# A three-product split of the first mixer's output projection on one Trainium2 core

## The reference, cut to what matters

```
def bidirectional(h, s_f0, s_b0):
    q, k, v, r, g_f, g_b = project(h)
    o_f, s_f = gla_chunk_scan(q, k, v, g_f, s_f0)
    o_b, s_b = gla_chunk_scan(flip_seq(q), flip_seq(k), flip_seq(v), flip_seq(g_b), s_b0)
    o = head_rms_norm(o_f + flip_seq(o_b), norm_g)
    return (o * jax.nn.silu(r)) @ w_out, s_f, s_b
...
lat = lat + (mod_l[:, 2] * rms_norm(y_lat, norm_g[i, 1])).astype(lat.dtype)
h = modulate(rms_norm(lat, norm_g[i, 2]), mod_l[:, 3], mod_l[:, 4])
lat = lat + (mod_l[:, 5] * rms_norm(swiglu(h, ffn_w_in[i], ffn_w_out[i]), norm_g[i, 3])).astype(lat.dtype)
```

## Time and profile before

| what | value |
|---|---|
| median of 3 runs | 1257.98 us (1257.1 to 1258.12) |
| the profiled execution's own time | 1255.89 us |
| its span, first to last instruction | 1253.6 us |
| mean granted TensorE clock | 0.989 of full speed |
| PE busy | 1190.9 us, 95% of the span |
| VectorE (DVE) busy | 730.1 us, 58% |
| ScalarE (ACT) busy | 538.2 us, 43% |
| GpSimd (POOL) busy | 38.7 us, 3% |
| HBM read | 207.86 MB, 167 GB/s over the span |

### The profile page before, as it was taken

How to read it: one execution, slowest core, us unless ns; L and a number is a source line. 1 busy time by engine, 2 the same in 40 slices (tenths; PEclk the granted TensorE clock), 3 DMA queues, 4 the chain that set the end, 5 groups by cost and what they waited for, 6 DMA issues and landing times.

```text
span 1253.6 us, 18595 instructions
## 1 busy us (share of the span) xinstructions
PE 1190.9 (95%) x7327; PEld 1009.3 (81%) x7327; DVE 730.1 (58%) x969; ACT 538.2 (43%) x715; POOL 38.7 (3%) x54
## 2 busy tenths in 40 slices
PE   3899998989999989999999999999999999999997
PEld 1477785479999978646899998999999985999996
DVE  1569335265555557664555456777777765654553
ACT  3762121253433453553343245555555544533442
POOL 2000010000000061000000000000000000000000
PEclk9998999999999989999999999999999999999999
DMA  9673470799655560425655543555555354746510
GB/s 319 235 275 107 167 268 7 246 244 281 199 156 150 184 172 5 184 85 197 208 198 176 200 110 107 146 152 151 151 147 134 76 200 160 256 154 206 179 65 34
DMA packets 201037, 209.70 MB, mean 167 GB/s; under 512 B 5803, under 2 KB 166838, under 8 KB 200790
## 3 DMA queue, kind: packets, MB, share of 16 engines
q1 hardware_dynamic: 197520, 201.61, 50.7%
q0 software_dynamic: 1648, 5.03, 1.6%
q10 hardware_dynamic: 1814, 2.30, 0.5%
HBM read 207.86 MB, written 2.01 MB: 167 GB/s over the span
## 4 chain that ended last, share of the span: by engine, by line
PE 87%; DVE 6%; DMA 3%; ACT 2%; issue 2%; DVEq 0%; SPq 0%; ACTq 0%
PE bank L1915 21%; PE bank L1916 20%; PE bank L1917 20%; PE bank L1713 3%; PE bank L1714 3%; PE bank L1715 3%; DMA weight_pool<-in_mod_w_dram 2%; PE bank L2129 2%; PE bank L1867 2%; PE bank L2270 2%; PE bank L2258 1%; PE bank L2248 1%; PE bank L1670 1%; DVE work L1435 1%; PE bank L2239 1%
## 5 line engine op out<-in xcount | busy, mean ns | idle before, releaser
L1915 PE MATMUL bank<-hT_high,mlp_up_high 128*128 128x256 f32 x512 | 145.2, 284 | 1.1 <-DVE hT_low L1337 1.1
L1917 PE MATMUL bank<-hT_high,mlp_up_low 128*128 128x256 f32 x512 | 144.9, 283 | 0.0
L1916 PE MATMUL bank<-hT_low,mlp_up_high 128*128 128x256 f32 x512 | 144.9, 283 | 0.0
L1915 PE MATMUL bank<-od_w_high,hT_high 128*128 128x384 f32 x384 | 132.7, 346 | 1.6 <-DVE hT_low L1337 1.4
L1917 PE MATMUL bank<-od_w_high,hT_low 128*128 128x384 f32 x384 | 128.7, 335 | 0.0
L1916 PE MATMUL bank<-od_w_low,hT_high 128*128 128x384 f32 x384 | 128.4, 334 | 0.0
L1041 DVE TENSOR_TENSOR mlp_down_low<-weight_pool,mlp_down_high 128x2048 fp32r<-128x2048 f32 x32 | 73.3, 2290 | 59.1 <-ACT mlp_down_high L620 59.1
L1915 PE MATMUL bank<-hT_high,ffn_up_high 128*128 128x256 f32 x352 | 99.8, 284 | 1.5 <-DVE hT_low L1041 1.5
L1915 PEld LDWEIGHTS bank<-hT_high,mlp_up_high 128*128 128x128 f32 x512 | 98.1, 192 | 2.9 <-issue 2.0
L1915 PE MATMUL bank<-mlp_down_high,hidden_high 128*128 128x512 f32 x256 | 99.9, 390 | 0.0
L1916 PE MATMUL bank<-mlp_down_low,hidden_high 128*128 128x512 f32 x256 | 99.9, 390 | 0.0
(11 more groups left out here) (311 smaller groups left out, 2589.7 us busy)
## 6 DMA issues: line engine op xcount, KB each, us to landing
weight_pool<-in_mlp_w_dram SPq DMA_DIRECT2D x64, 1024.0 KB, 7.5
weight_pool<-in_od_w_in_dram SPq DMA_DIRECT2D x72, 512.0 KB, 5.2
weight_pool<-in_mod_w_dram SPq DMA_DIRECT2D x22, 1024.0 KB, 9.8
weight_pool<-in_ffn_w_in_dram SPq DMA_DIRECT2D x44, 512.0 KB, 5.8
weight_pool<-in_gla_w_in_dram SPq DMA_DIRECT2D x12, 1024.0 KB, 6.5
weight_pool<-in_ffn_w_out_dram SPq DMA_DIRECT2D x22, 512.0 KB, 7.1
weight_pool<-in_gla_w_out_dram SPq DMA_DIRECT2D x2, 2048.0 KB, 15.4
weight_pool<-in_ev_w_in_dram SPq DMA_DIRECT2D x4, 1024.0 KB, 7.3
```

The lines of the kernel that those rows point to most:

```text
L1915: mm(out_, left[0], right[0], start=start, stop=False, **flag)
L1916: mm(out_, left[0], right[1], start=False, stop=False, **flag)
L1917: return mm(out_, left[1], right[0], start=False, stop=stop, **flag)
```

## The change

The output product takes the split form.

- **Activations.** `ogT` becomes `ogT2`, a high and a low half. ScalarE copies each of the banks 4 to 7 whole (512 columns) into the high half, VectorE subtracts for the low half.
- **Weights.** ScalarE makes the high halves of eight slices of 1024 columns: k 0 to 4 once the scores are done (`sT_ps` 4) and the weights have landed, k 5 to 7 after the last `state_updates` (`upd_ps` 8), since their place in `hT` holds `keT` until then. GpSimd makes the low halves of k 0 to 5, VectorE those of k 6 and 7. The low halves overwrite the raw weights.
- **Product.** 96 instructions with the same order of k and banks as before. PE waits for `ogT_lo`, `go_lo` and `go_lo_dve` in place of `ogT_act`, `ogT_dve` and the landings.
- **Places.** The two FFN weight sets change places (set 0 now at word 0), since the new halves lie in `work` at 8192 to 15360. So `ev_c` half 1 shares its place with the set of the last block, and is split after the last up product and no longer in the block before.

The diff, cut to its core, has in this order the places, GpSimd (ahead of `gate_rows(0)`), ScalarE (ahead of the squares, then the end of the FFN), VectorE (in place of `turn_evac`) and TensorE. Left out are the planner's entry that reserves words 16384 to 18431 of the pool for two high halves, VectorE's like edit at the end of the FFN, and `split_mm`, which only stands earlier in the code.

```
+        ogT2 = [view(over(f"mixed_{w}", "work", at, 2048), 0, KD, SEQ) for w, at in (("high", 8192), ("low", 12288))]
+        GO_HIGH = [("weight_pool", 16384), ("weight_pool", 17408), ("work", 10240), ("work", 11264), ("work", 14336), ("hT", 1024), ("hT", 2048), ("hT", 3072)]
+        goL = [over(f"gla_out{k}_low", "weight_pool", 8192 + D * k, D) for k in range(KD)]
...
-               for j, at in enumerate((10240, 0))]
+               for j, at in enumerate((0, 10240))]
...
+            for k in range(6):
+                g.wait_ge(s["go_hi"], k + 1)
+                e = L["go", k // 4]
+                g.tensor_tensor(goL[k][:, :], pool[:, e.at + D * (k % 4):e.at + D * (k % 4) + D], goH[k][:, :].bitcast(F32), ALU.subtract)\
+                 .then_inc(s["go_lo"], 1)
...
+            act.wait_ge(s["sT_ps"], 4)
+            for k in range(5):
+                gla_out_high(k)
+            act.wait_ge(s["upd_ps"], 8)
+            for k in range(5, KD):
+                gla_out_high(k)
...
-                if f >= FFC - 3 and f < FFC - 1:
-                    half = f - (FFC - 3)
+                if f == FFC - 3 or f == FFC - 1:
+                    half = (f - (FFC - 3)) // 2
                     if half:
-                        act.wait_ge(s["ff_ps"], FFC - 1)
+                        act.wait_ge(s["ff_ps"], FFC)
...
+            for k in (6, 7):
+                dve.wait_ge(s["go_hi"], k + 1)
+                e = L["go", 1]
+                low(goL[k][:, :], pool[:, e.at + D * (k - 4):e.at + D * (k - 4) + D], goH[k][:, :], "go_lo_dve")
+            for b in range(4):
+                dve.wait_ge(s["ogT_hi"], b + 1)
+                low(ogT2[1][:, 2 * b:2 * b + 2, :], bank[4 + b][:, :].rearrange("p (k t) -> p k t", k=2), ogT2[0][:, 2 * b:2 * b + 2, :], "ogT_lo")
...
-            out_product(0, [("go", 0), ("go", 1)], ogT)
+            for k in range(4):
+                pe.wait_ge(s["ogT_lo"], k // 2 + 1)
+                pe.wait_ge(s["go_lo"], k + 1)
+                for b in range(4):
+                    ins = out_part(k, b)
+            ins.then_inc(s["out_used"], 1)
+            pe.wait_ge(s["ogT_lo"], 4)
+            pe.wait_ge(s["go_lo"], 6)
+            pe.wait_ge(s["go_lo_dve"], 2)
+            for b in range(4):
+                for k in range(4, KD):
+                    ins = out_part(k, b)
+                if b == 1:
+                    ins.then_inc(s["y_half"], 1)
```

85 lines of the change are left out of this document (28 added, 57 removed).

## The result

The changed kernel takes 1249.10 us, median of 6 executions (1246.39 to 1251.43), beside 1257.08 us for the kernel before on the same chip (6 executions, 1256.31 to 1258.12): ratio 0.9935, 95% interval [0.9922, 0.9949], so 8.0 us or 0.65% faster. Its profiled execution took 1248.23 us (span 1246.3) at a mean granted clock of 0.992, where before's took 1255.89 at 0.989.

A forecast was written before the change was run, and what follows sets the result against it. PE, 87% of the chain of waits, was taken to bound the kernel. Terms -5.8 - 0.6 + 0.2 = -6.2 us, from a median of 1257.98, gave 1251.8 us, range 1249.6 to 1255.0.

The forecast's parts named there:

- The product: Mixer's output product on PE: 96 split instructions at 0.228 us take 21.9 us in place of 27.70, 5.8 us less.
- Its start: Output product's start on PE: 218.7 in place of 219.30 us, since ScalarE copies whole banks and VectorE subtracts, 0.6 us less.
- cover of VectorE's weight halves: VectorE's low halves k 6 and 7 finish 0.6 us before the first activation half; without that, product starts 0.4 us later.
- The weights' halves: Ahead of the output product: ScalarE's copies fit idle time and GpSimd's subtractions take 3.0 us each, costing 0.
- Late gate rows at 6 us each: If GpSimd's subtractions took 6 us, gate rows would be issued 12.7 us late, leaving 1 to 2 us on the path.
- Behind the product: Modulation slices 10 and 11 after the output product: late weights come near, loss 0.2 us, bounds 0 and 1.3.
- The end of the FFN: `ev_c` half 1 split behind the last block: ScalarE and VectorE work covered by 0.6 and 1.0 us, costing nothing.
- The sum: Whole kernel: product, its start and the loss behind it add to -6.2 us.
- The clock rival: PE's low-clock stretches move; two microseconds at the lower level are one on the path: 1250 to 1254 us, chance 0.15.
- VectorE blocked by GpSimd: GpSimd's subtractions hold VectorE's state updates at L1229: 1263.3 us, chance 0.05; milder form 1255 to 1257 us, chance 0.05.
- Late weights as the bound: Modulation slices 10 and 11 arrive 1 to 3 us after PE wants them: 1253 to 1255 us, chance 0.1.
- The pace of the split form: Output product's split instructions fall to the plain form's 0.433 us each, 41.6 us in all: 1271 us, chance 0.01.

The follow-up runs named there:

- `e_best`: Changed kernel with VectorE's weight subtractions ahead of the norm, modulation slices 10 and 11 fetched before the second FFN block, zero products in PE's waits: 1245.78 us.
- `e_side`: Kernel before plus the change's weight-half work on ScalarE, GpSimd and VectorE, PE waiting for it but the product still plain: 1256.43 us, ratio 0.9991.
- `e_pool2`: Changed kernel with a second, idle subtraction of 1024 columns on GpSimd ahead of each of its six: 1248.39 us, ratio 0.9928 to the kernel before.
- `a_again`: The changed kernel run once more, unaltered, beside many executions of the kernel before on the same chip: 1249.72 us, ratio 0.9946.
- `e_order`: Changed kernel with VectorE's weight subtractions ahead of the norm and modulation slices 10 and 11 fetched before the second FFN block: 1246.57 us, ratio 0.9929.
- `e_swap`: Kernel before with only the places changed: FFN weight sets exchanged, turned activations moved, `ev_c` half 1 split behind the last block: 1255.84 us, ratio 0.9999.
- `e_early`: Changed kernel with VectorE's two weight subtractions moved ahead of the norm's reductions: 1248.93 us, ratio 0.9946 to the kernel before.
- `b_plain`: The kernel before, run again unaltered as a control: 1255.03 us, ratio 1.0003.
- `a_plain`: The changed kernel, run again unaltered as a control: 1249.84 us, ratio 0.9961 to the kernel before.
- `a_warm`: Changed kernel with products of zeros filling PE's waits in six places: 1246.46 us, ratio 0.9931 to the kernel before.

## Where the prediction held, and where it did not

- **The product: -5.8.** Right: -5.65 us in the profile (27.63 to 21.98), at the FFN's pace of 0.227 us.
- **Its start: -0.6.** Right for the case that I read, the low clock at the turn: -0.64 (4.45 to 3.81). At the high clock it is -0.16 (3.15 to 2.99). I took the length of the turn, 3.43 us, for a fixed number. It was the clock's, and with it went the 0.6 us of cover of VectorE's weight halves. I had named the cover and its price (0.4 us), but not the thing that takes it away. By `e_best` the cover is worth 0.2 us; the other 0.24 are before's shorter start.
- **The weights' halves: 0.** Right, by `e_side` (0.1 us at the low clock, ratio 0.9991 [0.9973, 1.0009]). My 3.0 us for a subtraction was 0.65 too much, and even the lower bound, 2.4, lay a little above what was measured.
- **Late gate rows at 6 us each: a loss of 1 to 2.** Not as I put it. `e_pool2` issued them about 2.8 us late, without loss. A delay of 12.7 us, the case that I had priced, was not tried.
- **Behind the product: +0.2.** Too small: 0.42 us in the first profile, 0.84 in `a_again`. I had let slice 11 land by 243.6 with the queue as it was before. The earlier issue, with the same full DMA engines ahead of it, only lengthened its way from 8.8 to 11.8 us. Then the FFN's input comes another 0.4 us later: its 16 transposes (L1652) took 3.24 us in one piece in after's profile, in a low-clock stretch from 247.5 us, and 1.06 and 1.09 us in `e_order`, where no such stretch stood and nothing waited for slice 11. Before had the same stretch (255.4 to 258.8), but it began 1.7 us behind the first transpose in place of 0.8, and from the product's start to the FFN's input it cost 0.1 us there, beside `e_swap`, which had none. The wait for slice 11 isn't needed for the stretch: `e_early` and `e_pool2` had it without the wait. Why it begins earlier in the changed kernel stays open.
- **The end of the FFN: 0.** Right, by the rows above and by `e_swap`.
- **The sum: -6.2.** The stage gives 5.50 us with the low clock at the turn, 4.2 for `b_plain` and `a_plain`, and 5.2 with the clock held up. The medians give 6.1 over all executions, about 5 at the clocks where both kernels have many, and 4.7 for the pair with the zero products. At the low clock the 0.7 us that are missing are 0.2 of slice 11, 0.4 of the FFN's input and 0.15 of the product. With the clock held up the 1.0 us are 0.4 of slice 11 (0.58 in `a_warm`, for my 0.2), 0.4 of the start and 0.15 of the product. That -6.2 agrees to 0.1 us with the medians over all executions is luck in part. The terms summed to less, and the changed kernel's executions had slightly more of the full clock (a mean of 0.9907 against 0.9898), which is worth 0.4 to 0.9 us by the two lines. Why they had isn't settled.
- **The step that failed** is "The median of the runs lies 2.1 us above that execution, so I forecast 1257.98 - 6.2 = 1251.8 us". The median of three was 2.4 us too high a base, and the range left only 2.2 us below the forecast. The three executions of before lay in the upper part of a range that reaches from 1251.7 to 1261.2 us. The profiled execution, 1255.89, was near the median of 70, 1255.6. From it the forecast would have been 1249.7, which is within 0.2 us of the changed kernel's 1249.5. The clock rival named the mechanism but priced it for this stage alone, at 2 us. Over the program it moves one unchanged kernel by 9 us. Beside the six executions of the first comparison (1257.08) the base was 0.9 us too high and the change 1.8 us too small; that their 1257.08 is itself 1.5 us above the 70 is the part whose cause stays open.
- **The rivals.** VectorE blocked by GpSimd: not so, 3.22 to 3.23 us in all groups. The Trainium skill ("SBUF — State Buffer", section Who interferes with whom) lets the two engines contend when VectorE's instruction has two SBUF inputs and GpSimd's reads SBUF. The trace agrees with the reading that a bank and a column of factors don't count, and the two weight subtractions of `e_early`, which have two SBUF inputs, took 2.63 us beside GpSimd and 2.36 elsewhere. Late weights as the bound: not for slice 10 (2.4 us to spare), for 0.4 to 0.8 us on slice 11, which holds the stage in the changed kernel's first profile, `a_plain`, `a_again` and `a_warm`. The pace of the split form: as in the FFN.

## What to carry to other kernels

Where a plain float32 product of this size is bound by PE, three rounded products take 80% of its time (21.98 to 27.63 us), if the other engines have idle time for the halves; look for that time in their timelines ahead of the product, and give the late halves to whichever engine waits there anyway. Before a difference of less than 1% is believed, look at how wide the unchanged kernel ranges and at the granted clock of each execution, and base a forecast on many executions or on the stage, not on the median of three. And a duration that was read in a low-clock stretch is no constant: ask what it hides, and what is late when it is gone.

## What was not expected of the hardware

- **The clock as the largest term.** 43 products of zeros in PE's waits took 4.4 us off the kernel before (1255.55 to 1251.14, ratio 0.9970 [0.9960, 0.9980]) and 3.4 off the changed one (1249.84 to 1246.46). In the executions of before, each 0.001 of mean granted clock goes with 1.0 us, in those of the changed kernel with 0.5.
- **GpSimd.** A subtraction of 1024 columns with two inputs takes 2.33 to 2.39 us, less than twice the 1.48 of 512 columns that ran beside VectorE instructions with two SBUF inputs. With the same input twice it took 1.90 us.
- **One small transfer in the way of all.** While GpSimd's write of the gate rows (1024 numbers) is under way, some 10 us, one issue on SP takes 8.7 to 10.1 us in each of the 14 profiles. In 13 of them it is the third issue of the FFN's weights; in `e_pool2`, where the write comes 2.8 us later, it is the sixth. The transfers are held too. Two of 512 KB, issued 1.3 us behind the write, landed after a median of 14.1 us in the changed kernel, while the DMA engines moved 38 GB/s at most in any 2 us up to 218 us, and after 6.2 us in `e_pool2`, where they went 1.4 us ahead of it and 203 to 267 GB/s flowed. What holds them isn't shown.
